# The first half's decays of a state scan computed inside the mixer before it, and unread constant products at five places

## The reference, cut to what matters

```
r, k, v, lora = token_shift(h @ w_in_r)            # 15 blocks of 128 rows
log_w[d] = -exp(-0.5) * sigmoid(w0[d] + tanh(lora_w[d]) @ w2[d])
a[d]     = sigmoid(a0[d] + lora_a[d] @ a2[d])      # the rates
k_hat    = normalize(k * k_k);   k[d] = k * (1 + (a[d] - 1) * k_a)
S <- S * w - (S @ k_hat)(k_hat * a) + v k[d]       # the scan, 64 tokens a chunk
y = sum_d S @ r;  out = (group_norm(y) + bonus(r, k, v)) * gate(lora_g)
```

## Time and profile before

| | us |
|---|---|
| median of 3 runs (lowest, highest) | 2600.43 (2599.57, 2600.64) |
| the profiled execution's own time | 2601.43 |
| its span, first to last instruction | 2599.5 |
| mean granted TensorE clock | 0.974 |
| busy: TensorE, VectorE, ScalarE | 2427.9, 1456.4, 878.2 |

### The profile page before, as it was taken

The page is one execution under the profiler, slowest core; times in us unless marked ns, Lnnn a source line. Parts: engine busy times, 40 slices in busy tenths (PEclk is TensorE's granted clock), DMA queues, the critical chain, the costliest instruction groups (busy, mean ns, idle before and its releaser), DMA issues.

```text
span 2599.5 us, 42266 instructions
## 1 busy us (share of the span) xinstructions
PE 2427.9 (93%) x17846; PEld 1972.7 (76%) x17846; DVE 1456.4 (56%) x2326; ACT 878.2 (34%) x1491; POOL 76.8 (3%) x148
## 2 busy tenths in 40 slices
PE   8999999999999999667877999999999999999998
PEld 6777778688887767567766688877788877777997
DVE  5555565655554578666544555545655554563553
ACT  2341132422222435633224422222422222454543
POOL 0000000000000000000000000000000000000000
PEclk9999999999999999788988999999999999999999
DMA  7236525344444310000003344344344443202543
GB/s 295 103 114 215 190 98 210 139 145 133 144 138 146 132 65 33 1 4 4 4 4 129 108 144 139 137 140 146 126 138 145 136 145 124 93 34 85 189 180 130
DMA packets 55916, 310.95 MB, mean 120 GB/s; under 512 B 5936, under 2 KB 9392, under 8 KB 28080
## 3 DMA queue, kind: packets, MB, share of 16 engines
q1 hardware_dynamic: 32944, 224.75, 24.3%
q0 software_dynamic: 20736, 75.51, 8.9%
q10 hardware_dynamic: 2048, 7.98, 0.8%
HBM read 307.16 MB, written 1.05 MB: 119 GB/s over the span
## 4 chain that ended last, share of the span: by engine, by line
PEld 42%; PE 28%; issue 13%; DVE 11%; ACT 5%; PEldq 0%; DMA 0%; DVEq 0%; SPq 0%; ACTq 0%
PEld bank L1423 14%; PEld bank L1416 13%; PEld bank L1419 12%; PE bank L1265 5%; PE bank L1262 2%; PE bank L1324 2%; PE bank L1340 2%; PE bank L1473 2%; PE bank L1080 1%; PE bank L1087 1%; PE bank L1083 1%; PE bank L1152 1%; PE bank L996 1%; ACT hn L1886 1%; DVE ms L2361 1%
## 5 line engine op out<-in xcount | busy, mean ns | idle before, releaser
L2374 DVE TENSOR_TENSOR w_lo<-ring,w_hi 128x1024 fp32r<-128x1024 f32 (+1 forms) x195 | 232.5, 1192 | 440.7 <-ACT w_hi L1849 440.7
L1416 PE MATMUL bank<-ffn_x_hi,w_hi 128*128 128x512 f32 x984 | 388.7, 395 | 0.0
L1419 PE MATMUL bank<-ffn_x_lo,w_hi 128*128 128x512 f32 x984 | 388.7, 395 | 0.0
L1423 PE MATMUL bank<-ffn_x_hi,w_lo 128*128 128x512 f32 x984 | 388.7, 395 | 0.0
L1849 ACT ACTIVATE w_hi<-ring 128x1024 fp32r<-128x1024 f32 (+1 forms) x195 | 200.5, 1028 | 281.7 <-PE bank L1419 271.0
L2303 DVE SCALAR_TENSOR_TENSOR ms<-mod_rows,c_silu 128x1024 f32<-128x1024 f32 x200 | 244.0, 1220 | 1.3
L1416 PEld LDWEIGHTS bank<-ffn_x_hi,w_hi 128*128 128x128 f32 x984 | 184.4, 187 | 45.4
L1423 PEld LDWEIGHTS bank<-ffn_x_hi,w_lo 128*128 128x128 f32 x984 | 184.4, 187 | 45.1
L1419 PEld LDWEIGHTS bank<-ffn_x_lo,w_hi 128*128 128x128 f32 x984 | 184.4, 187 | 45.1
L1416 PE MATMUL bank<-ffn_h_hi,w_hi 128*128 128x512 f32 x528 | 213.4, 404 | 0.0
L1423 PE MATMUL bank<-ffn_h_hi,w_lo 128*128 128x512 f32 x528 | 208.6, 395 | 0.0
(11 more groups left out here) (437 smaller groups left out, 4696.9 us busy)
## 6 DMA issues: line engine op xcount, KB each, us to landing
ring<-in_stream SPq DMA_DIRECT2D x211, 1024.0 KB, 4.8
mod_rows<-in_mod_stream POOLq DMA_DIRECT2D x144, 512.0 KB, 3.8
one_const<-in_one ACTq DMA_DIRECT2D x1, 1665.0 KB, 14.0
mix_const<-in_two ACTq DMA_DIRECT2D x1, 1440.0 KB, 6.2
win_const<-in_win ACTq DMA_DIRECT2D x1, 1216.0 KB, 5.3
x<-in_x SPq DMA_DIRECT2D x4, 256.0 KB, 4.7
c_silu<-in_c SPq DMA_DIRECT2D x1, 1024.0 KB, 10.1
x<-in_x SPq DMA_DIRECT2D x1, 1024.0 KB, 25.6
```

The costliest lines, as they stand in the source:

```text
L1416: mm = pe.matmul(bank[:, 0:tok], w_high, hi, start=k == 0, stop=False)
L1419: mm = pe.matmul(bank[:, 0:tok], w_high, lo, start=False, stop=False)
L1423: mm = pe.matmul(bank[:, 0:tok], w_low, hi, start=False, stop=last)
L2374: V.tensor_tensor(low[:, 0:h.nk, :], raw_half(h), high[:, 0:h.nk, :].bitcast(F32), ALU.subtract).then_inc(sem("w_split"), 1)
```

## The change

- `BLENDS`: the shifted halves come as lora, k, r, v.
- `FEATURES_AFTER`: `blend(0)` now holds for hf = 1 the lora functions and the w2 rates (after the work of place 9), the sums (places 11 to 16), the a2 rates (16), `steps` (the four scale-and-add instructions that stood in `exps`; 17, 18), `exps` (18, 19), the decays of d = 0 and `bonus_in` (19) and the decays of d = 1 (20). Each has its place at the end of that place's event on all engines. TensorE's rates wait for the Tanh (`lora_ready`).
- ScalarE takes the first of the three instructions of `shift`; it waits for the half's bank, and VectorE waits for it (`kept`).
- The rates are made for one half of the tokens at a time: 8 events of two 256-column products for each half. Those of hf = 0, with `vt` of 2 and 3 and `steps`, go into `late`, now 42 items over 57 steps from step 1.
- `keep_busy` takes a count and a width, and is also called at the first scan step, in advance(3) before x, u and state, in `readout(0)`, at the start of both `mixer` stages and at the start of `project_parts`.
- Buffers move: hf = 1 and hf = 0 of the scan's operands have homes of their own (`at_pair`).

```diff
-LATE_FROM, LATE_OVER, OUT_FROM = 3, 54, 95
+LATE_FROM, LATE_OVER, OUT_FROM = 1, 57, 95
...
-          ... [("w_in_r", j) for j in (6, 7, 2, 3, 4, 5, 0, 1)],
+          ... [("w_in_r", j) for j in (6, 7, 2, 3, 0, 1, 4, 5)],
+FEATURES_AFTER = {
+    9: [("lora",), *(("rates", "w2", d, 1, g) for d in range(2) for g in range(2)), ("exp_table",)],
+    11: [("sums", 0, 1, n) for n in range(2)], 12: [("sums", 0, 1, n) for n in range(2, 4)],
+    13: [("sums", 0, 1, 4), ("sums", 1, 1, 0)], 14: [("sums", 1, 1, n) for n in range(1, 3)],
+    15: [("sums", 1, 1, n) for n in range(3, 5)],
+    16: [("sums", 1, 1, 5), *(("rates", "a2", d, 1, g) for d in range(2) for g in range(2)), ("exp_table",)],
+    17: [("steps", 0, 1)], 18: [("exps", 0, 1), ("steps", 1, 1)],
+    19: [("exps", 1, 1), *(("decay", 0, 1, n) for n in range(6)), ("bonus_in", 1)],
+    20: [("decay", 1, 1, n) for n in range(6)]}
...
-            yield from (("rates", "w2", 0, 0), ("rates", "w2", 1, 0), ("rates", "a2", 0, 1), ("rates", "a2", 1, 1))
-            sums, products = decays(1)
...
-            yield from (("rates", "a2", 0, 2), ("rates", "a2", 1, 2), ("vt", 2), ("vt", 3))
...
+            rates = [("rates", w, d, 0, g) for w in ("w2", "a2") for d in range(2) for g in range(2)]
+            late = [("vt", 2), ("vt", 3), ("bonus", 1), ("vt", 0), ("vt", 1), *rates, ("bonus_in", 0), *sums[0], ("bonus", 0),
+                    *sums[1][0:2], ("steps", 0, 0), ("exps", 0, 0), *sums[1][2:], *products[0][0:2], ("steps", 1, 0), ("exps", 1, 0),
+                    *products[0][2:], *products[1]]
...
+            def keep_busy(bank, times=WARM, cols=3 * P):
...
+            def rates(w, d, hf, g):
+                rows = by_head(d)
+                bank, full = take_bank()
+                pe.wait_ge(sem("lora_ready"), 1)
+                for k in range(2):
+                    m = 2 * g + k
+                    mm = pe.matmul(bank[:, k * SEQ:(k + 1) * SEQ], s2(w)[rows, m * P:(m + 1) * P],
+                                   ph3["lora"][rows, int(w == "a2"), half_cols[hf]], start=True, stop=True)
+                mm.then_inc(full, 1)
...
                 for c, h in enumerate(parts_out):            # project_parts
+                    bank, full = take_bank()
+                    if c == 0:
+                        keep_busy(bank, 16)
                     pe.wait_ge(sem("w_split"), b_w + c + 1)
...
                     bank, full = take_bank()                 # mixer, dense
+                    if h == 0:
+                        keep_busy(bank, (5, 4)[layer])
...
+                    if hf == 0 and g == 0 and what != "gate":   # readout
+                        keep_busy(bank, 2 if what == "centre" else 3, 2 * P)
...
-                            pe.wait_ge(sem(f"decayed{d}"), 1 + i // 2)
+                                if (i, d, name) == (0, 0, "lw"):    # tokens
+                                    keep_busy(bank, 8)
+                                pe.wait_ge(sem(f"decayed{d}"), 1 + i // 2)
...
+                    if i == 3 and what != "y":               # x, u, state; before their waits
+                        keep_busy(bank[0], 2, 2 * P)
...
                     if h.kind == "shift":                    # ScalarE, blend
-                        shifted[h.c] = turns.next()
+                        bank, _ = full_bank()
+                        shifted[h.c] = (turns.n - 1) % BANKS, (turns.n - 1) // BANKS
+                        act.wait_ge(sem("keep_ready"), 1)
+                        nc.scalar.activation(rec_chunks[h.c], bank[:, :], ACT.Copy, scale=keep[:, h.c:h.c + 1]).then_inc(sem("kept"), 1)
...
-                link(V.tensor_scalar(d3, b3, keep[:, c:c + 1], None, ALU.mult))
+                kept[0] += 1
+                dve.wait_ge(sem("kept"), kept[0])
```

More of the change, by code:

```diff
@@ L315, in blend_order @@
                 yield "pair", i
-        if layer == 0 and at == 19:
-            yield "lora", 0
+        if layer == 0:
+            for event in FEATURES_AFTER.get(at, ()):
+                yield "feature", event
 class Step:
@@ new lines, in build, with at_pair @@
+        sig = [[own[2], whole(rstd2[:, :, :])], [y_sum[:, :, 0:SEQ], whole(hn[:, 6:8, :])]]
+        step_of = [homes[0]["lw"], sig[1]]
+        bonus_of = [inc1, whole(ms2[:, :, :])]
+        def at_pair(d, name, pair):
+            return homes[d][name][pair // 2][:, :, pair % 2 * P:(pair % 2 + 1) * P]
+        two_of = lambda t: [t[:, 0, :], t[:, 1, :]]
+        idle = [tmp[:, :], *(ph3["temps"][:, k, :] for k in range(2, 8)), *(ph3["more"][:, k, :] for k in range(8)),
+                *(hn[:, k, :] for k in range(4)), c2("cos2"), c2("sin2"), *two_of(rs2), *two_of(rstd2),
+                *(free_slots[2][:, k * TOK:(k + 1) * TOK] for k in range(4)),
+                *(free_slots[1][:, k * TOK:(k + 1) * TOK] for k in range(2, 4))]
@@ new lines, in bonus_in, with feature @@
+            def bonus_in(hf):
+                cols = half_cols[hf]
+                for m in range(4):
+                    last = V.scalar_tensor_tensor(bonus_of[hf][:, m, :], ph3["r"][:, m, cols], param("r_k", m), ph3["k"][:, m, cols],
+                                                  ALU.mult, ALU.mult)
+                link(last)
+                dve.nop().then_inc(sem("bonus_in"), 1)
+            def feature(what, *how):
+                if what == "rates":
+                    turns.next()
+                elif what == "sums":
+                    summed_logs(*how)
+                elif what == "decay":
+                    decay(*how)
+                elif what == "bonus_in":
+                    bonus_in(*how)
@@ L2935, in recurrence @@
                             step(d, *how)
-                    elif what == "rates":
-                        for m in range(4):
-                            turns.next()
-                    elif what == "sums":
-                        sums(*how)
-                    elif what == "decay":
-                        decay(*how)
+                    elif what in ("rates", "sums", "decay", "bonus_in"):
+                        feature(what, *how)
                     elif what == "vt":
                         turns.next()
-                    elif what == "bonus_in":
-                        bonus_in(*how)
                     elif what == "bonus":
```

254 lines of the change are left out of this document (124 added, 130 removed).

## The result

| | before | after |
|---|---|---|
| median (all runs), us | 2600.53 (2599.57 to 2600.89) | 2632.01 (2614.20, 2631.03, 2632.99, 2633.16) |
| ratio after / before, 95% interval | | 1.0096 [1.0076, 1.0116] |
| the profiled execution, its span, its granted clock | 2601.43, 2599.5, 0.974 | 2614.20, 2612.3, 0.977 |

The change makes the kernel slower by 31.5 us in the median; the forecast of 2611.5 had the sign, and 2632 lies outside its range. The runs lie on two levels some 18 us apart, and the profile was taken of the one execution on the lower level. (The ratio in the table is the recorded one and counts both levels; the medians alone give 1.0121.) So it has to be read twice: at its own level it says whether the steps of the forecast hold, and what lifts the other three runs it can't show.

What follows compares the result with a forecast made beforehand. TensorE bounds blend, no engine alone the scan. Pre-scan −1.4, late items +5, advance(3) −3, readout +0.5, project_parts +7.2, mixers +3.2 and −0.4: +11.1 on 2601.4, 2612.5; as median 2611.5, range 2595 to 2621.

Steps and rivals of the forecast that it cites:

- the second rival: Scan: the clock stays up, three fewer restarts of 3 us each, −9, 2602.5 us, no change; chance 0.17.
- step 8: Start of the mixers: constant products cost +3.2 us in layer 0, with inputs ready, and give −0.4 in layer 1.
- step 6: advance(3) and readout: constant products keep off half clock, −3 us in advance(3); +0.5 in the readout.
- Steps 1 and 2: Blend: rates wait 7.3 us for the Tanh, take 3.6, restart at half clock costs 3.0; half 18 ends at 1066.6.
- Step 3: End of blend: VectorE's tail of 22.3 us behind half 18, all in front of the barrier, ends at 1088.9.
- the first rival: Inserted work is free: Tanh stall and cold restart (10.3), late weights (2.0) and step 5's 5 us vanish; 2594.2 us; chance 0.15.
- Step 4: First scan step: eight constant products behind the barrier, scan starts at 1097.2 at full clock; pre-scan −1.4 us.
- Step 5: Scan: late items add 9 us of TensorE and 11 of ScalarE; taken as +5 us, bounds nothing and 12.
- Step 7: Front of project_parts: sixteen constant products behind the barrier at half clock delay the real work, +7.2 us.
- VectorE as the bound of the scan: Scan: 26 us of late work in 37 steps instead of 47 makes VectorE the bound; 2620 us; chance 0.15.
- Constant products covered: First scan step, project_parts, mixers: idle time covers the products, −5, −10 and −6; 2590 us; chance 0.03.

Runs made afterwards that it cites:

- no_fill: The change without any of its constant products at the five new places: 2599.9 us, ratio 0.9994 to the kernel before.
- early_tanh: The change without its new constant products, and with the rates one place behind the Tanh (place 10 for 9): 2594.2 us, ratio 0.9978 to the kernel before.
- no8: The change without the eight constant products in front of the scan's first step, the others kept: 2607.3 us, ratio 1.0024 to the kernel before.
- only16: The change with only the sixteen constant products in front of project_parts, none at the other new places: 2604.8 us, ratio 1.0012 to the kernel before.
- early_again: Repeat of `early_tanh` on another call's chip: 2597.5 us, ratio 0.9984 to the kernel before.

## Why the forecast was wrong

**The place that failed is the sum's treatment of the clock.** It priced each restart at about 3 us, from the 6 us at half rate behind the pauses of the earlier trace rows, and nowhere let a restart cost more. Of the pauses inside the scan it said only that fewer falls would help (the second rival). The upper level pays for 44 us at half clock in one place: in the repeated change's profile, 16 of the 19 us that separate it from the lower one, nearly the distance from 2614 to 2632. The three upper runs of the result were not profiled; their times and mean clocks (0.968 and 0.969) are those of that one (0.969). No step names prepare(0)'s pause, and the upper bound of 2621 was made of VectorE's late work, not of the clock.

On its own level the account gives 2612.5 for the profiled execution, and that took 2614.2. That this is so close is in part luck. By the steps the scan starts 4.4 us later than before (1.6 by steps 1 to 4, 2.8 by step 8), is 0.5 shorter, and project_parts costs 7.2: 11.1. Measured are 1.2 later, 4.4 longer and 7.1. Two errors of 3 and 5 us stand against each other: the start came sooner, and what the warm start and step 6 were to give back inside the scan didn't come.

**Steps 1 and 2 (blend).** Right. Stall 6.52 us (7.3 forecast); rates 5.62 us, at half clock, which lasts some 9 us from the restart at 968.92 (6 forecast). The Tanh follows its table load by 0.01 us, and the load the instruction before it by 0.02; the Trainium skill ("ScalarE: Activation LUTs", "What ACT_TABLE_LOAD costs") has about 1.4 us of drain there as well, which this row doesn't show; by that figure, as an estimate, the forecast's 7.3 would have been 8.7. Half 9 starts 11.2 us late (963.3 to 974.5; 13.9 forecast). Half 18 ends at 1066.6, the forecast's number, though 0.6 us of it come from blend's later start.

**Step 3.** Right: VectorE's last decay ends at 1089.2 (1088.9). In `no_fill` the scan starts 206.5 us behind blend's first plain product (`ring,hn`), before 212.3: the moved decays bring 5.8 of the 35 us, and the longer scan takes them back. What steps 1 and 2 cost is shown by `early_tanh`: 0.16 % against `no_fill`, 0.10 % the second time (3 to 4 us), of the 10.3 that the first rival gave.

**Step 4.** As forecast against the kernel before: scan from 1096.78 (1097.2), at full clock. But against its own alternative it is a loss that the forecast never set up: without the eight the change starts the scan 7.4 us sooner (205.5 for 212.9 from that product of blend), and `no8` is at 2607.3 where the change's lower level is 2611 to 2614. The eight cost 4 to 7 us there, and they put the pause of prepare(0) where the upper level begins.

**Step 5, late items.** Within its bounds but not to be had as one number. From the first `tokens` to the end of the gate before takes 283.2 us; with the late items in the scan and no product there 290.0 (`no_fill`), 284.5 (`only16`), 283.7 (`early_tanh`) and 287.5 (`early_again`), with the same code. The scan varies by more than the +5 in question.

**Step 6.** Wrong in its time, right about the clock: −3 and +0.5 forecast, nothing found. From x of the last quarter to the end of the gate it is 41.5 us before and 41.5 after (1342.94 to 1384.40), and 41.1 in `no_fill`. The waits behind the products are 0.53 and 0.50 us where they were 1.54 and 1.51, and the granted clock over the stretch is 0.91, for 0.79 before and in `no_fill`; over the last 41.5 us of the scan it is 0.87 to 0.95 in all eight profiles with these products and 0.76 to 0.82 in the ten without. What failed is the step from clock to time: TensorE is busy 28.8 of the 41.5 us (24.2 before), and the stretch is as long as it was.

```profile
1337.24:1378.74 41.50, 24.21 (x532) 0.79 0.25 103
1342.94:1384.40 41.46, 28.84 (x559) 0.91 0.27 103
```

(The first is the kernel before, the second the change.)

**Step 7.** Right: from the gate's end to the last high-by-high product 62.7 us for 55.6, +7.1 (+7.2). **Step 8.** Right for layer 0: from the lam product to the third half tile (37.45) 21.2 us for 18.2, +3.0 (+3.2; the sum takes back 3.0 where the earlier trace rows give 2.8). Layer 1's four fitted its wait. Blend starts only 0.6 us later than before (883.9 for 883.3), so 1.8 us were made up on the way; in the repeated change it is 887.5, so one profile doesn't settle it.

**The rivals.** Free inserted work: no, the Tanh stall stood; with it out of the way, and no constant products, 2594 to 2598 was measured. VectorE as the bound of the scan (2620): not seen at the lower level; in the window of the earlier trace rows VectorE is now busy 10.2 us, TensorE 16.6. Constant products covered: no. The clock in the scan was the right subject with the wrong sign.

**What stays open.** Whether taking the 3.1 us pause away would end the matter: products ahead of it only moved it, and no kernel without it was tried. Whether large products right behind it bring the clock back once it has fallen 0.2 to 1.2 us behind it, as the levels say and no profile shows. And why half clock lasts 44 us on a busy engine. The Trainium skill ("TensorE: Matmul & The Clock Gate", "What's actually happening") says that one and the same kernel runs another number of matmuls cold from run to run, by its phase against the clock's control. The two levels of one kernel agree with that in kind; in size the profiles show 3.4 to 44.4 us at half clock at the same pause.

## To carry to other kernels

Work that keeps an engine's clock up is only free inside a wait that the profile shows, behind the same barrier as the work it stands in front of, and even there a higher clock is not yet time (step 6). Put ahead of data that is ready it costs more than the warm start gives back: net 7.1 and 3.0 us here in project_parts and layer 0. Price a pause not by its usual restart alone: look at every pause near which the clock falls, take two or three profiles, and try the kernel with one product more or less before believing a gain or loss of under 1 %. Find every inserted instruction in the trace before reading its time: four experiments here had theirs on the other side of the pause than intended, and mean something else than their expectations say. When a unit of work is moved into a busy stage, give the engine that prepares its input one event's head start; here that one line (the rates one place behind the Tanh) was worth 3 to 4 us and made the moved decays a gain of about 0.2 %.

## What the runs showed of the hardware

TensorE was at 1.2 GHz (granted 0.50) for 44.4 us while busy for 43 to 44 of them, where the same instructions in other runs had 2.4 GHz after 3.4 to 10.2 us. It came behind one pause of 3.1 us, in three profiles in which the clock fell 0.2, 0.5 and 1.2 us after the pause's end. Six products of 384 columns beginning 1.8 us behind that pause took the upper level away in 18 of 18 executions, where it had stood in 12 of 15; no profile shows how. A kernel's level depended on shifts of about 1 us: eight, seven and ten constant products in front of the scan gave 2621, 2613 to 2627 and 2609 us, and four products in a stage 800 us earlier, with a few behind the place, 2612 for 2594. Six groups of constant products in the scan's last quarter went with a granted clock of 0.87 to 0.95 there, in place of 0.76 to 0.82, and took nothing off the 41.5 us of that stretch in the change.
